# Low parts of the second weights: from VectorE subtractions to negated copies and adding transfers inside SBUF

## The chip, the cores and the metric

One core of a Trainium2 chip runs the whole kernel. The metric is the device time of one execution in microseconds (us); lower is better. The kernel before has a median of 1407.5 us over three executions.

## What is computed

Two transformer blocks in a row, each over 512 tokens of width 1024 (the second one has 16 more meta tokens inside it). Around the change only the MLP of each block matters:

```python
# first block
x = x + jnp.square(jax.nn.relu(h2 @ w_mlp_in[layer])) @ w_mlp_out[layer]
# second block
def squared_relu_mlp(u, w_ff1, w_ff2):
    hdn = jnp.square(jax.nn.relu(jnp.einsum('bld,df->blf', u, w_ff1)))
    return jnp.einsum('blf,fd->bld', hdn, w_ff2)
```

`w_mlp_in` and `w_ff1` are 1024 x 4096, `w_mlp_out` and `w_ff2` 4096 x 1024. The other parts (two attentions, a gated linear attention, norms, gates) are untouched.

## The kernel before, in words

**Split operands.** Every float32 operand of TensorE is kept as a high part (a copy rounded to `fp32r`) and a low part (operand minus high part). A product is three matmuls: high x high, high x low, low x high. So each weight costs an ACT copy (high part) and a VectorE subtraction (low part): `wh`, `wl` for what is read straight from a weight, `Sh`, `Sl` for blocks of the second weight.

**The MLPs.** Each of the two MLPs goes through the hidden dimension in 4 chunks of 1024. The last chunk of each is done in another way; the first three run in a loop on every engine (`strassen_chunk`), and only these are changed. One such chunk has two stages:

- *Slab stage*: 8 products of the first weight, each 24 matmuls of 128x512 (`products`, L2355). The last of them belongs to the next chunk.
- *Pair stage*: 4 pairs, q = 0 to 3, each 256 columns of the second weight. A pair is 7 block products in Strassen's manner (`block_product`, L2420), each 12 matmuls of 128x256, in this order: A11, S1, S2, S3, S4, A12, A22. A11, A12 and A22 are blocks of the weight itself; S1 to S4 are sums of blocks. A12 and A22 together are the pair's lower half, and A11 its upper left block.

So there are 2 MLPs x 3 chunks x 4 pairs = 24 pairs.

**Who makes what.** The raw weights (1 MB for two slabs or for a pair) come by SP's transfers into `raw`, which has two slots. A slot is loaded again when `lo_ready` says that the low parts of what lay in it are done (`mlp_loads`, L663). The sums S1 and S3 are made by GpSimd's queue: `s13_sums` issues two plain transfers of 256 KB (L824), waits for them (`s13_base`), and issues two adding transfers of 256 KB on top (L827). It runs for unit u = 4c + q, and waits first until the S1 and S3 of unit u - 2 have been split (`s13_lo`, the VectorE instruction L1550). S2 and S4 are VectorE additions (L1535, L1541).

The lower half of a pair is split by ACT L988 (high part, 128x1024, `hi_ready`) and VectorE L1568 (low part, `lo_ready`). ACT may start on it when the pair before has ended (`slab_done`), because `wh[:, 1]` is still read by that pair's A12 and A22. TensorE waits for it only ahead of A12. The upper left block is split by ACT L968 (`a11_hi`) and VectorE L1545 (`a11_lo`); it is needed at the start of a pair.

ACT, VectorE, GpSimd and SP each work through a program in fixed order, written by hand, with waits on semaphores; GpSimd's is `strassen_sums`.

Of the kernel before, what the change touches and what calls it, by code (L numbers as in the profile page):

```python
# [23 lines left out]
F32 = mybir.dt.float32  # L24
# [9 lines left out]
DM = 1024  # L34
# [137 lines left out]
def build(nc, d):  # L172
# [21 lines left out]
    with ctx:  # L194
# [41 lines left out]
        def region(at, *shape):  # L236
# [126 lines left out]
            sem("blk_done"), sem("mid_read"), sem("mids_zero"), sem("x_combined"))  # L363
        a11_hi, a11_lo, s13_hi, s13_lo = sem("a11_hi"), sem("a11_lo"), sem("s13_hi"), sem("s13_lo")
        s2_hi, s2_lo, s4_hi, s4_lo = sem("s2_hi"), sem("s2_lo"), sem("s4_hi"), sem("s4_lo")
        s13_base, s2_sum, s4_sum = sem("s13_base"), sem("s2_sum"), sem("s4_sum")
        s13_sum = sem("s13_sum0"), sem("s13_sum1")
        hid_sq, t_diff, t4_diff, hid_hi, hid_lo = (
            sem("hid_sq"), sem("t_diff"), sem("t4_diff"), sem("hid_hi"), sem("hid_lo"))
        g_landed, ts_sum, ts3_sum = sem("g_landed"), sem("ts_sum"), sem("ts3_sum")  # L370
        tw_hi, tw_lo, y_t = sem("tw_hi"), sem("tw_lo"), sem("y_t")
# [88 lines left out]
        def lower_pair(p):  # L460

            return raw[:, p % 2, :].rearrange("p (k n) -> p k n", k=KT)[:, 4:8, :].rearrange("p k (o n) -> p o k n", o=2)

        def lower_slot(w):

            return w[:, 1, :].rearrange("p (o k n) -> p o k n", o=2, k=4)

# [247 lines left out]
        def _(pool):  # L715
# [47 lines left out]
            def strassen_sums(which):  # L763
                t0, _, p0 = MLPS[which]
                pool.memset(mids, 0.0).then_inc(mids_zero, 1)
                if which == REAL:
                    add_squares(3, REAL)
                for c in range(CHUNKS - 1):
                    for q in range(4):
                        s13_sums(which, c, q)  # L770
                if which == REAL:
                    first_token_sum()
                pool.wait_ge(evac_done, t0 + 16 * (CHUNKS - 1))
                x = X[:, :, META:S2].rearrange("p (q o) (t n) -> p q o t n", o=2, t=2)
                n = 4 if which == REAL else 0
                pool.tensor_tensor(x[:, :, 0, 1], x[:, :, 0, 1], mids[:, :, 0:HB], ALU.add).then_inc(x_combined, 1)
                pool.tensor_tensor(x[:, :, 1, 0], x[:, :, 1, 0], mids[:, :, 0:HB], ALU.subtract).then_inc(x_combined, 1)
                pool.tensor_tensor(x[:, :, 1, 1], x[:, :, 1, 1], mids[:, :, 0:HB], ALU.subtract).then_inc(x_combined, 1)
                pool.wait_ge(x_combined, n + 3)
                pool.tensor_tensor(x[:, :, 1, 1], x[:, :, 1, 1], mids[:, :, HB:2 * HB], ALU.subtract).then_inc(x_combined, 1)  # L780
                pool.wait_ge(x_combined, n + 4)
                if which == REAL:
                    token_sums()

            def add_block(upper, left, accumulate, landed):
# [114 lines left out]
        def _(act):  # L900
# [52 lines left out]
            def strassen_chunk(which, c):  # L953
# [12 lines left out]
                def upper_left(q):  # L966
                    act.wait_ge(w_landed[(p0 + 4 + q) % 2], landed_count(p0, 4 + q) + 64 * c)
                    act.activation(blk(Sh[:, 0:S1]), quarter(p0 + 4 + q, 0, 0), ACT.Copy).then_inc(a11_hi, 1)  # L968

# [17 lines left out]
                def lower(q):  # L987
                    act.activation(lower_slot(wh), lower_pair(p0 + 4 + q), ACT.Copy).then_inc(hi_ready, 2)  # L988

# [448 lines left out]
        def _(dve):  # L1438
# [78 lines left out]
            def strassen_chunk(which, c):  # L1517
# [24 lines left out]

                def upper_left(q):
                    dve.wait_ge(a11_hi, pairs + q + 1)
                    dve.tensor_tensor(blk(Sl[:, 0:S1]), quarter(p0 + 4 + q, 0, 0), blk(Sh[:, 0:S1]),  # L1545
                                      ALU.subtract).then_inc(a11_lo, 1)

                def first_sums(q):
# [16 lines left out]

                def lower(q):
                    dve.wait_ge(hi_ready, t + 8 + 2 * q + 2)
                    dve.tensor_tensor(lower_slot(wl), lower_pair(p0 + 4 + q), lower_slot(wh), ALU.subtract)\  # L1568
                       .then_inc(lo_ready, 2)

# [9 lines left out]
                for j in range(8):  # L1580
# [25 lines left out]
                    else:  # L1606
# [6 lines left out]
                                                 op0=ALU.mult, op1=ALU.subtract).then_inc(t4_diff, 1)  # L1613
                        if j == 6:
                            upper_left(0)
                        if j == 7:
# [4 lines left out]
                        if j == 7:  # L1621
# [3 lines left out]
                                          hidden_part(Hh, k, T4, 3), ALU.subtract).then_inc(hid_lo, 1)  # L1625
                    if j == 7:
                        lower(0)

                for q in range(4):
                    g1, g2, g3, g4 = pair_banks(q)  # L1630
                    done, last = blocks + 6 * q, q == 3
                    x0, x1 = X[:, 2 * q, META:S2], X[:, 2 * q + 1, META:META + HB]
                    mid = halves(mids[:, q])
                    if q > 0:
                        first_mids(q)
                    dve.wait_ge(blk_done, done + 4)
                    dve.wait_ge(mid_read, reads + 2 * q + 1)
                    dve.tensor_tensor(mid, mid, ps[:, g2:g4 + 1, 0:HB], ALU.add).then_inc(mid_read, 1)
                    if last:
                        slab_weights(p0, 0, t + 17)  # L1640
                    else:
                        upper_left(q + 1)
                        second_sum(q + 1)
                        fourth_sum(q + 1)
                        first_sums(q + 1)
                    dve.wait_ge(blk_done, done + 6)
                    dve.tensor_tensor(halves(x0), halves(x0), ps[:, g1:g3 + 1, 0:HB], ALU.add)
                    if not last:
                        last_low(q + 1)
                    dve.wait_ge(slab_done, t + 8 + 2 * q + 2)  # L1650
                    dve.tensor_tensor(x1, x1, ps[:, g4, 0:HB], ALU.subtract).then_inc(evac_done, 2)
                    if last:
                        slab_weights(p0, 1, t + 18)
                    else:
                        lower(q + 1)

# [681 lines left out]
        def _(pe):  # L2338
# [66 lines left out]
            def strassen_chunk(which, c):  # L2405
# [4 lines left out]
                upper, lower = slice(0, S1), slice(S1, DM)  # L2410
                A12_, A22_ = (blk(wh[:, 1, upper]), blk(wl[:, 1, upper])), (blk(wh[:, 1, lower]), blk(wl[:, 1, lower]))
                S4_, S2_ = (blk(wh[:, 0, upper]), blk(wl[:, 0, upper])), (blk(wh[:, 0, lower]), blk(wl[:, 0, lower]))
# [16 lines left out]
                for q in range(4):  # L2429
                    g1, g2, g3, g4 = pair_banks(q)  # L2430
                    pe.wait_ge(a11_lo, pairs + q + 1)
                    if q == 0:
# [23 lines left out]
                    block_product(S4_, B22, g3, False, all_ready).then_inc(blk_done, 1)  # L2456
                    pe.wait_ge(lo_ready, t + 8 + 2 * q + 2)
                    block_product(A12_, B21, g1, False).then_inc(blk_done, 1)
# [529 lines left out]
```

## Time and profile before

| what | value |
|---|---|
| median of 3 executions | 1407.5 us (1407.33 to 1407.54) |
| the profiled execution, first to last instruction (span) | 1405.3 us |
| median less that span | 2.2 us |
| TensorE busy | 1397.8 us, 99% of the span |
| VectorE busy | 921.2 us, 66% |
| ACT busy | 596.3 us, 42% |
| GpSimd busy | 211.8 us, 15% |
| mean traffic | 115 GB/s, 161.61 MB |

The profiled execution has no separately recorded time; its span stands for it, and the 2.2 us between span and median are taken as a constant that lies around the span. Durations of single instructions overlap: a matmul of 128x256 is shown with 0.28 us, but the next one starts 0.12 us after it. So distances are read from starts, not from durations.

### The profile page before, as it was taken

What the parts mean: (1) busy time and instruction counts of PE and PEld (TensorE: products, weight loads), DVE (VectorE), ACT (ScalarE), POOL (GpSimd) and SP (SyncE); (2) the same over time, 40 slices, a digit from 0 to 9 for tenths busy, and PEclk for the clock granted to TensorE, in tenths of its full rate; (3) what the DMA queues carried; (4) which work ended last, traced back from release to release, by engine and by line L of the source; (5) the groups of instructions that cost most, each with busy time, mean ns of one, the idle gap of its engine ahead of it and who ended that gap; (6) DMA issues with size and microseconds to landing.
All of it is one profiled execution on the core that took longest, in us unless ns stands there. A gap on an engine that the chain in (4) does not pass through costs nothing.

```text
span 1405.3 us, 21789 instructions
## 1 busy us (share of the span) xinstructions
PE 1397.8 (99%) x8746; PEld 1184.5 (84%) x8746; DVE 921.2 (66%) x1248; ACT 596.3 (42%) x842; POOL 211.8 (15%) x215
## 2 busy tenths in 40 slices
PE   9999999999999999999999999999999999999998
PEld 7898779777888989989888997778888998989886
DVE  6635433765767858577656778556756967758775
ACT  4324531553445434353244435344434535344353
POOL 4000000000022302211433020000022221302310
PEclk9999999999999999999999999999999999999999
DMA  5223123211336845635233322232225773927573
GB/s 183 90 91 113 61 68 102 72 31 59 100 99 169 188 133 144 157 114 153 91 96 99 92 63 82 64 103 90 90 90 139 180 162 113 214 91 191 138 175 109
DMA packets 154860, 161.61 MB, mean 115 GB/s; under 512 B 4010, under 2 KB 144660, under 8 KB 154788
## 3 DMA queue, kind: packets, MB, share of 16 engines
q1 hardware_dynamic: 122868, 129.12, 28.9%
q0 software_dynamic: 31904, 31.46, 12.3%
q8 instruction: 53, 0.87, 0.3%
q14 instruction: 19, 0.16, 0.0%
q10 hardware_dynamic: 16, 0.00, 0.0%
HBM read 157.68 MB, written 2.10 MB: 114 GB/s over the span
## 4 chain that ended last, share of the span: by engine, by line
PE 99%; ACT 0%; DVE 0%; issue 0%; POOL 0%; POOLq 0%; ACTq 0%
PE ps L2355 63%; PE ps L2420 17%; PE ps L2351 4%; PE ps L2377 4%; PE ps L2493 3%; PE ps L2748 1%; PE ps L2563 1%; PE ps L2777 1%; PE ps L2763 1%; PE ps L2867 1%; PE ps L2652 0%; PE ps L2695 0%; PE ps L2674 0%; PE ps L2949 0%; PE ps L2540 0%; PE ps L2713 0%
## 5 line engine op out<-in xcount | busy, mean ns | idle before, releaser
L2355 PE MATMUL ps<-AA,wh 128*128 128x512 f32 x1440 | 453.5, 396 | 0.0
L2355 PE MATMUL ps<-BB,wh 128*128 128x512 f32 x1088 | 342.2, 396 | 0.2 <-issue 0.2
L2355 PEld LDWEIGHTS ps<-AA,wh 128*128 128x128 f32 x1440 | 267.4, 188 | 62.6 <-DVE wl L1449 0.8
L2355 PE MATMUL ps<-AA,wl 128*128 128x512 f32 x720 | 283.4, 394 | 0.0
L915 ACT ACTIVATE wh<-raw 128x1024 fp32r<-128x1024 f32 (+2 forms) x149 | 141.5, 950 | 259.8 <-PE ps L2355 206.0
L2355 PEld LDWEIGHTS ps<-BB,wh 128*128 128x128 f32 x1088 | 202.2, 188 | 49.3 <-issue 1.6
L2355 PE MATMUL ps<-BB,wl 128*128 128x512 f32 x544 | 213.9, 393 | 0.0
L1449 DVE TENSOR_TENSOR wl<-raw,wh 128x1024 fp32r<-128x1024 f32 (+2 forms) x149 | 169.9, 1140 | 60.6 <-ACT wh L915 60.3
L2355 PEld LDWEIGHTS ps<-AA,wl 128*128 128x128 f32 x720 | 135.4, 188 | 30.9
L2355 PEld LDWEIGHTS ps<-BB,wl 128*128 128x128 f32 x544 | 102.3, 188 | 23.3
L2420 PE MATMUL ps<-Hl,wh 128*128 128x256 f32 x384 | 107.8, 281 | 0.0
L1494 DVE TENSOR_TENSOR arena<-ps,RS 128x512 f32<-128x512 f32 (+2 forms) x55 | 37.9, 689 | 73.1 <-PE ps L2355 69.2
L1526 DVE TENSOR_TENSOR wl<-raw,wh 128x1024 fp32r<-128x1024 f32 x48 | 62.2, 1296 | 31.6 <-ACT wh L963 16.5
L2420 PE MATMUL ps<-Hl,Sh 128*128 128x256 f32 x288 | 81.1, 282 | 0.0
L2420 PEld LDWEIGHTS ps<-Hl,wh 128*128 128x128 f32 x384 | 72.3, 188 | 0.0
L963 ACT ACTIVATE wh<-raw 128x1024 fp32r<-128x1024 f32 x36 | 38.1, 1060 | 62.0 <-PE ps L2355 62.0
L1588 DVE SCALAR_TENSOR_TENSOR zf<-ps,RS 128x512 f32<-128x512 f32 x48 | 33.2, 691 | 44.9 <-PE ps L2355 44.2
L2420 PEld LDWEIGHTS ps<-Hl,Sh 128*128 128x128 f32 x288 | 54.2, 188 | 0.2
L2420 PE MATMUL ps<-AA,wh 128*128 128x256 f32 x192 | 54.3, 283 | 0.0
L2420 PE MATMUL ps<-AA,wl 128*128 128x256 f32 x192 | 53.8, 280 | 0.0
L2420 PE MATMUL ps<-BB,wl 128*128 128x256 f32 x192 | 53.7, 280 | 0.0
L2420 PE MATMUL ps<-BB,wh 128*128 128x256 f32 x192 | 53.7, 280 | 0.0
(408 smaller groups left out, 2410.6 us busy)
## 6 DMA issues: line engine op xcount, KB each, us to landing
raw<-in_w_in SPq DMA_DIRECT2D x38, 1024.0 KB, 5.4
raw<-in_w_ff SPq DMA_DIRECT2D x31, 1024.0 KB, 5.4
raw<-in_w_mlp_in SPq DMA_DIRECT2D x16, 1024.0 KB, 5.4
raw<-in_w_mlp_out SPq DMA_DIRECT2D x16, 1024.0 KB, 5.3
zf<-in_w_mlp_out POOLq DMA_DIRECT2D x48, 256.0 KB, 4.8
zf<-in_w_ff POOLq DMA_DIRECT2D x48, 256.0 KB, 4.6
raw<-in_w_out SPq DMA_DIRECT2D x8, 1024.0 KB, 5.4
arena<-in_x SPq DMA_DIRECT2D x4, 512.0 KB, 7.1
```

Source lines behind the costliest of these rows:

```text
L915: act.activation(w_slab(wh, t % 2, kt), raw_slab(t), ACT.Copy).then_inc(hi_ready, 1)
L963: act.activation(w_slab(wh, j % 2, KT), raw_half((p0 + i) % 2, j % 2, KT, 2), ACT.Copy)\
L1449: dve.tensor_tensor(w_slab(wl, t % 2, kt), raw_slab(t), w_slab(wh, t % 2, kt), ALU.subtract)\
L1494: dve.tensor_tensor(tokens(dst, kind), dense_psum(t, kind)[0:rows], tokens(scale, kind), ALU.mult)\
L1526: dve.tensor_tensor(w_slab(wl, slot, KT), raw_half(p % 2, slot, KT, 2), w_slab(wh, slot, KT), ALU.subtract).then_inc(lo_ready, 1)
L1588: dve.scalar_tensor_tensor(out=f, in0=halves(dense_psum(t0 + j, which)), scalar=0.0, in1=halves(RS[:, 0:S1]), op0=ALU.max, op1=ALU.mult).t ...
L2351: last = pe.matmul(dense_psum(t_ps, ALL)[:, half, :], a[:, k, :], b[:, o0 + k, half * HALF2:(half + 1) * HALF2], start=start, stop=stop)
L2355: last = pe.matmul(dense_psum(t_ps, kind), a[:, k, :], b[:, o0 + k, col0:col0 + S1], start=start, stop=stop)
L2377: mm = pe.matmul(ps[:, value_banks(t) + a // 2, a % 2 * 256:a % 2 * 256 + 256], x, w[:, k, :], start=(half == 0 and k == 0 and i == 0 and ...
L2420: mm = pe.matmul(ps[:, bank, 0:HB], w[:, k, :], hidden_part(x, k, b), start=(first and k == 0 and i == 0), stop=(k == 3 and i == 2), skip_ ...
L2493: mm = pe.matmul(ps[:, bank, :], x, v[:, k, :], start=(first and k == 0 and n == 0), stop=(k == 3 and n == 2), skip_group_check=True)
L2563: return pe.matmul(dense_psum(t, ONE), w_slab(w, t, KT)[:, k, :], x[:, k, 0:S1], start=first, stop=last)
```

## The change

Low parts of the lower half and of the upper left block are no longer VectorE subtractions. ACT writes, beside the high part, a second copy with scale -1 into the place of the low part (so that `wl` or `Sl` holds minus the high part, rounded as it is), and GpSimd's queue adds the raw weight onto it by a transfer from SBUF to SBUF with `accumulate`. The lower half keeps the layout of `raw` now, so that a partition's 1024 elements are one run on both sides; TensorE picks A12 and A22 out with a stride. The adding transfers are new entries in GpSimd's fixed order: after the sums of unit u come the lower half of unit u - 2 and the upper left block of unit u - 1. TensorE waits for their landings (`a11_landed`, `lower_lo`), and VectorE waits for `lower_lo` too, to pass it on as `lo_ready` to SP.

```diff
+        neg_hi, lower_lo = sem("neg_hi"), sem("lower_lo")
+        neg_a11, a11_landed = sem("neg_a11"), sem("a11_landed")
...
         def lower_pair(p):
-            return raw[:, p % 2, :].rearrange("p (k n) -> p k n", k=KT)[:, 4:8, :].rearrange("p k (o n) -> p o k n", o=2)
-
-        def lower_slot(w):
-
-            return w[:, 1, :].rearrange("p (o k n) -> p o k n", o=2, k=4)
+            return raw[:, p % 2, DM:2 * DM]
+
+        def lower_block(w, o):
+
+            return w[:, 1, :].rearrange("p (k o n) -> p o k n", o=2, k=4)[:, o]
...
                 for c in range(CHUNKS - 1):
                     for q in range(4):
                         s13_sums(which, c, q)
+                        if 4 * c + q >= 2:
+                            lower_low(which, 4 * c + q - 2)
+                        if 4 * c + q >= 1:
+                            upper_left_low(which, 4 * c + q - 1)
+                lower_low(which, 4 * (CHUNKS - 1) - 2)
+                upper_left_low(which, 4 * (CHUNKS - 1) - 1)
+                lower_low(which, 4 * (CHUNKS - 1) - 1)
...
+            def upper_left_low(which, u):
+                pool.wait_ge(neg_a11, so_far(which, 4) + u + 1)
+                pool.dma_start(blk(Sl[:, 0:S1]).bitcast(F32), quarter(MLPS[which][2] + 4 + u % 4, 0, 0), accum_op=ALU.add)\
+                    .then_inc(a11_landed, 16)
+
+            def lower_low(which, u):
+                pool.wait_ge(neg_hi, so_far(which, 4) + u + 1)
+                pool.dma_start(wl[:, 1, :].bitcast(F32), lower_pair(MLPS[which][2] + 4 + u % 4), accum_op=ALU.add).then_inc(lower_lo, 16)
...
                 def upper_left(q):
                     act.wait_ge(w_landed[(p0 + 4 + q) % 2], landed_count(p0, 4 + q) + 64 * c)
+                    act.activation(blk(Sl[:, 0:S1]), quarter(p0 + 4 + q, 0, 0), ACT.Copy, scale=-1.0).then_inc(neg_a11, 1)
                     act.activation(blk(Sh[:, 0:S1]), quarter(p0 + 4 + q, 0, 0), ACT.Copy).then_inc(a11_hi, 1)
...
                 def lower(q):
-                    act.activation(lower_slot(wh), lower_pair(p0 + 4 + q), ACT.Copy).then_inc(hi_ready, 2)
+                    act.activation(wh[:, 1, :], lower_pair(p0 + 4 + q), ACT.Copy).then_inc(hi_ready, 2)
+                    act.activation(wl[:, 1, :], lower_pair(p0 + 4 + q), ACT.Copy, scale=-1.0).then_inc(neg_hi, 1)
...
-                def upper_left(q):
-                    dve.wait_ge(a11_hi, pairs + q + 1)
-                    dve.tensor_tensor(blk(Sl[:, 0:S1]), quarter(p0 + 4 + q, 0, 0), blk(Sh[:, 0:S1]),
-                                      ALU.subtract).then_inc(a11_lo, 1)
...
-                def lower(q):
-                    dve.wait_ge(hi_ready, t + 8 + 2 * q + 2)
-                    dve.tensor_tensor(lower_slot(wl), lower_pair(p0 + 4 + q), lower_slot(wh), ALU.subtract)\
-                       .then_inc(lo_ready, 2)
+                def lower_landed(q):
+                    dve.wait_ge(lower_lo, 16 * (so_far(which, 4) + q + 1) + 64 * c)
+                    dve.sem_inc(lo_ready, 2)
...
                     else:
-                        upper_left(q + 1)
                         second_sum(q + 1)
                         fourth_sum(q + 1)
                         first_sums(q + 1)
+                    lower_landed(q)
                     dve.wait_ge(blk_done, done + 6)
...
-                A12_, A22_ = (blk(wh[:, 1, upper]), blk(wl[:, 1, upper])), (blk(wh[:, 1, lower]), blk(wl[:, 1, lower]))
+                A12_, A22_ = ((lower_block(wh, o), lower_block(wl, o)) for o in range(2))
...
-                    pe.wait_ge(a11_lo, pairs + q + 1)
+                    pe.wait_ge(a11_hi, pairs + q + 1)
+                    pe.wait_ge(a11_landed, 16 * (so_far(which, 4) + q + 1) + 64 * c)
...
-                    pe.wait_ge(lo_ready, t + 8 + 2 * q + 2)
+                    pe.wait_ge(lower_lo, 16 * (so_far(which, 4) + q + 1) + 64 * c)
                     block_product(A12_, B21, g1, False).then_inc(blk_done, 1)
```

**GpSimd's queue.** Before, from the sums of unit 2 of the first MLP on (L824 are the plain, L827 the adding transfers of `s13_sums`):

```order
L824 DMA zf<-in_w_mlp_out 128x4x128 [waits s2_sum,s13_lo]
L824 DMA zf<-in_w_mlp_out 128x4x128
L827 DMA zf<-in_w_mlp_out 128x4x128 [waits s13_base]
L827 DMA zf<-in_w_mlp_out 128x4x128
L824 DMA zf<-in_w_mlp_out 128x4x128 [waits s2_sum,s13_lo]
```

In the changed kernel the same place (L842 and L845 are these transfers now; L796 is the upper left block, L801 the lower half):

```order
L796 DMA Sl<-raw 128x4x128 [waits neg_a11]
L842 DMA zf<-in_w_mlp_out 128x4x128 [waits s2_sum,s13_lo]
L842 DMA zf<-in_w_mlp_out 128x4x128
L845 DMA zf<-in_w_mlp_out 128x4x128 [waits s13_base]
L845 DMA zf<-in_w_mlp_out 128x4x128
L801 DMA wl<-raw 128x1024 [waits neg_hi]
L796 DMA Sl<-raw 128x4x128 [waits neg_a11]
L842 DMA zf<-in_w_mlp_out 128x4x128 [waits s2_sum,s13_lo]
```

Each unit has two more transfers with a wait of their own, and they stand behind the four transfers of a later unit's sums and behind the wait in their midst.

**VectorE, end of the slab stage and first pair.** Before, from the last hidden low part to the reading of the middle results of pair 0 (L1568 is the lower half's low part of pair 0):

```order
L1624 TENSOR_TENSOR Hl<-zf,AA 128x768 [waits hid_hi]
L1567 REGISTER_ALU
L1568 TENSOR_TENSOR wl<-raw,wh 128x1024 [waits hi_ready]
L1636 REGISTER_ALU
L1638 TENSOR_TENSOR zf<-zf,ps 128x512 [waits mid_read,blk_done]
```

Changed, the same place and on to pair 0's results (L1648 was L1638, L1565 was L1550, L1656 is in `x0`'s line behind the wait for the landing, L1657 was L1647):

```order
L1636 TENSOR_TENSOR Hl<-zf,AA 128x768 [waits hid_hi]
L1646 REGISTER_ALU
L1648 TENSOR_TENSOR zf<-zf,ps 128x512 [waits mid_read,blk_done]
L1555 TENSOR_TENSOR zf<-zf,raw 128x512 [waits s13_sum1,w_landed1,s4_lo]
L1560 REGISTER_ALU [waits s4_lo]
L1561 TENSOR_TENSOR zf<-raw,zf 128x512 [waits s2_sum]
L1565 TENSOR_TENSOR Sl<-zf,Sh 128x1024 [waits s13_hi]
L1582 REGISTER_ALU
L1656 REGISTER_ALU [waits lower_lo]
L1657 TENSOR_TENSOR X<-X,ps 128x512 [waits blk_done]
```

The subtraction is gone, and a wait for the transfer's landing stands between the split of the next pair's S1 and S3 and the reading of this pair's results; what releases the slot of `raw` comes out of that wait.

## Rows read from the trace of the kernel before

**Rows 1.** Page, part 1: busy time, share of the span, instructions.

```profile
PE 1397.8 (99%) x8746; PEld 1184.5 (84%) x8746; DVE 921.2 (66%) x1248; ACT 596.3 (42%) x842; POOL 211.8 (15%) x215
```

**Rows 2.** Waits of TensorE: engine line <- releaser: us in total, times, longest.

```profile
PE ps L2555 <- POOL ident L726: 1.7, 1, 1.7
PE ps L2563 <- ACT AA L1169: 0.5, 1, 0.5
PE ps L2355 <- issue: 0.2, 1, 0.2
```

**Rows 3.** Stretches: us; busy of PE, PEld, DVE, ACT, POOL; PEclk; DMA share; GB/s.

```profile
460.00:470.00 10.00, 10.00 (x87) 10.00 (x86) 9.73 (x15) 6.51 (x9) 2.78 (x4) 1.00 0.75 159
480.00:490.00 10.00, 10.00 (x87) 10.00 (x86) 7.62 (x11) 3.19 (x3) 4.17 (x4) 1.00 0.94 212
500.00:510.00 10.00, 10.00 (x45) 8.11 (x44) 3.72 (x6) 3.30 (x5) 0.00 (x0) 1.00 0.33 105
```

**Rows 4.** Timeline of TensorE: start of pair 0, its A12, start of pairs 1 and 2.

```profile
457.65 0.28 PE L2420 MATMUL ps<-AA,Sh 128*128 128x256 f32 x1
...
464.76 0.28 PE L2420 MATMUL ps<-AA,wh 128*128 128x256 f32 x1
...
467.63 0.28 PE L2420 MATMUL ps<-AA,Sh 128*128 128x256 f32 x1
...
477.61 0.28 PE L2420 MATMUL ps<-AA,Sh 128*128 128x256 f32 x1
```

**Rows 5.** Timeline of ACT: high parts of the lower halves of pairs 0 and 2.

```profile
461.94 1.04 ACT L988 ACTIVATE wh<-raw 128x1024 fp32r<-128x1024 f32 x1
...
477.87 1.07 ACT L988 ACTIVATE wh<-raw 128x1024 fp32r<-128x1024 f32 x1 [0.53 <-PE ps L2420]
```

**Rows 6.** Timeline of VectorE: pair 0's lower half, pair 2's S1 and S3.

```profile
463.38 1.22 DVE L1568 TENSOR_TENSOR wl<-raw,wh 128x1024 fp32r<-128x1024 f32 x1
...
476.10 1.22 DVE L1550 TENSOR_TENSOR Sl<-zf,Sh 128x1024 fp32r<-128x1024 f32 x1
```

**Rows 7.** Timeline of GpSimd's queue, sums of units 3 and 4; idle time in brackets.

```profile
468.63 1.54 POOL L824 DMA_DIRECT2D zf<-in_w_mlp_out  x2 [7.22 <-DVE Sl L1550]
473.57 2.62 POOL L827 DMA_DIRECT2D zf<-in_w_mlp_out  x2 [3.39 <-DMA zf<-in_w_mlp_out]
477.62 1.54 POOL L824 DMA_DIRECT2D zf<-in_w_mlp_out  x2 [1.43 <-DVE Sl L1550]
```

**Rows 8.** Single lines: their issues (ns), and below each the time to landing.

```profile
L824 POOL DMA_DIRECT2D zf<-in_w_mlp_out x24: 777/778/1884, 419.2 to 638.2; - x24
...
DMA to landing us min/median/max: 3.3/3.5/10.6
...
L827 POOL DMA_DIRECT2D zf<-in_w_mlp_out x24: 1306/1562/1876, 425.7 to 642.8; - x24
...
DMA to landing us min/median/max: 4.2/5.3/10.7
...
L663 SPq DMA_DIRECT2D raw<-in_w_mlp_out x12: 372/373/382, 439.9 to 640.5; - x12
...
DMA to landing us min/median/max: 4.9/5.4/10.7
```

**Rows 9.** DMA queues, 470 to 490 us: packets, MB, share of 16 engines.

```profile
q0 software_dynamic: 2490, 2.32, 63.9%
q1 hardware_dynamic: 2080, 2.10, 31.9%
```

**Rows 10.** DMA queue of GpSimd, 1355 to 1367 us (one adding transfer of 1 MB).

```profile
q0 software_dynamic: 528, 1.05, 51.3%
```

**Rows 11.** VectorE's groups that the change removes: busy us, mean ns, idle.

```profile
L1568 DVE TENSOR_TENSOR wl<-raw,wh 128x1024 fp32r<-128x1024 f32 x24 | 29.2, 1217 | 0.0
...
L1545 DVE TENSOR_TENSOR Sl<-raw,Sh 128x512 fp32r<-128x512 f32 x24 | 16.4, 684 | 0.0
```

**Rows 12.** Waits of SP's queue.

```profile
SPq L663 <- DVE wl L1568: 197.0, 20, 14.9
```

More of the change, by code:

```diff
@@ L363, in build @@
             sem("blk_done"), sem("mid_read"), sem("mids_zero"), sem("x_combined"))
-        a11_hi, a11_lo, s13_hi, s13_lo = sem("a11_hi"), sem("a11_lo"), sem("s13_hi"), sem("s13_lo")
+        a11_hi, s13_hi, s13_lo = sem("a11_hi"), sem("s13_hi"), sem("s13_lo")
         s2_hi, s2_lo, s4_hi, s4_lo = sem("s2_hi"), sem("s2_lo"), sem("s4_hi"), sem("s4_lo")
@@ L1613, in strassen_chunk @@
                                                  op0=ALU.mult, op1=ALU.subtract).then_inc(t4_diff, 1)
-                        if j == 6:
-                            upper_left(0)
                         if j == 7:
@@ L1625, in strassen_chunk @@
                                           hidden_part(Hh, k, T4, 3), ALU.subtract).then_inc(hid_lo, 1)
-                    if j == 7:
-                        lower(0)
                 for q in range(4):
@@ L1653, in strassen_chunk @@
                         slab_weights(p0, 1, t + 18)
-                    else:
-                        lower(q + 1)
             def mlp_last():
```

## The prediction

> **What bounds the kernel now.** I read the page's busy times first, then TensorE's waits, then stretches of the pair stage, then the timelines of one pair engine by engine, and last the DMA queues. TensorE is busy for 1397.8 us of 1405.3 [rows 1], and all its waits in the whole program are 1.7, 0.5 and 0.2 us [rows 2]: none of them lies at the block products. In the pair stage it starts as many matmuls (x87 in 10 us) whether VectorE is busy for 9.73 or for 7.62 of the 10 us [rows 3]. So TensorE has nothing to gain from a freer VectorE, neither a wait nor pace. Whatever the change delays beyond its cover is added to the time, and nothing of it is made good later, as TensorE has no idle time to eat into.
>
> The cover is short. A pair starts at 457.65, its A12 at 464.76, the next pairs at 467.63 and 477.61 [rows 4]: a pair lasts 10.0 us, and the lower half is due 7.1 us after its start. ACT begins the high part of pair 0's lower half at 461.94, late, behind its work on the hidden parts; for pair 2 it begins at 477.87, 0.26 us into the pair [rows 5]. VectorE then has the low part of pair 0 done at 464.60, just ahead of 464.76 [rows 6].
>
> **What the change removes.** 24 subtractions of 1.217 us and 24 of 0.684 us on VectorE, 45.6 us of busy time [rows 11]. On the path they are worth nothing, as said. Their one effect is that pair q+1's S1 and S3 are split some 0.6 us earlier in pair q: now the split ends at 476.10 + 1.22 = 477.3, which is 9.7 us after the pair's start, then about 9.1.
>
> **What it adds on ACT.** Per pair a negated copy of 128x1024 (1.06 us, as the high part in rows 5) and one of 128x512. ACT is idle for over half of a pair stage's stretch, 3.19 busy of 10 us in the later pairs [rows 3], so they cost nothing on ACT itself, but the first one stands in series ahead of the transfer.
>
> **What it adds on the queues.** Per pair one adding transfer of 512 KB for the lower half and one of 256 KB for the upper left block. No row shows one from SBUF to SBUF. What it costs has two sides, engine time and landing.
>
> *Engine time.* In 470 to 490 us the loads took 31.9% of 20 us for 2.10 MB, the sums' queue 63.9% for 2.32 MB [rows 9]. A load of 1.05 MB is thus 3.2 us of all 16 engines, a pair's sums (1.05 MB) 5.8 us. Half of the sums is plain; at the loads' rate that half is 1.6 us, which leaves 4.2 us for the adding half, 8.0 us per MB. The one adding transfer of 1 MB, whose runs are 2 KB long instead of 512 B, took 51.3% of 12 us for 1.05 MB, 5.9 us per MB [rows 10]. The lower half has runs of 4 KB, so I take 5.9 for it: 0.52 MB, 3.1 us. The upper left block has runs of 512 B, so 8.0: 0.26 MB, 2.1 us. Bounds for the two: 1.6 and 0.8 us at the loads' rate, 4.2 and 2.1 at 8.0 us per MB.
>
> *Landing.* A load lands after 5.4 us [rows 8], 2.2 more than its 3.2 of engine time. So the lower half lands 2.2 + 3.1 = 5.3 us after its issue when nothing else runs; bounds 3.8 and 6.4. The nearest rows agree: 5.3 in the median for adding transfers of 256 KB two at a time, 3.5 for plain ones [rows 8]. The Trainium skill, "DMA: Bandwidth & Descriptors", section on the anatomy of one DMA on the SWDGE path, gives about 2.0 us plus bytes over 436 GB/s whatever the transfer does: 3.2 us for 512 KB. This trace contradicts it for adding transfers, whose 256 KB take longer than plain ones; by it the sum below would be 34 us instead of 86.
>
> **The sum, per chunk.** *Pair 0.* ACT's high part ends at 462.98, the negated copy at about 464.0, the landing at 469.3; A12 was due at 464.76. TensorE waits 4.5 us.
>
> *Pairs 1 to 3.* All 16 engines now have 3.2 (load) + 5.8 (sums) + 3.1 + 2.1 = 14.2 us of work per pair, against 9.0 before, where a pair lasts 10.0 and the DMA share was already 0.94 [rows 3]. GpSimd's order ties every pair to all of it: the lower half of unit u - 2 is issued behind unit u's sums. The same loop followed through the waits: from a pair's start 9.1 us to the split of S1 and S3, 1.5 for two plain issues, 3.4 until they land, 2.6 for two adding issues [rows 7], 5.3 for the landing of the next pair's lower half, 2.9 for A12 and A22. That is 24.8 us for two pairs, 12.4 for one, if nothing shares the engines. The larger one holds, about 14.1 us a pair: 4.1 us of waiting in each of three pairs, and 4.5 + 12.3 = 16.8 us in chunks 1 and 2 of each MLP.
>
> *Chunk 3* has no sums of a further chunk to issue, so the lower halves of its pairs 2 and 3 stand behind nothing. The landing is at 0.26 + 2.0 + 5.3 = 7.6 us into the pair, 0.5 late. Together 4.5 + 4.1 + 0.5 + 0.5 = 9.6 us.
>
> One MLP: 2 x 16.8 + 9.6 = 43.2 us; two: 86.4 us. Against the profiled span 1405.3 + 86.4 = 1491.7; the medians lie 2.2 above the span, so **1493.9**.
>
> Edits costed at nothing: the upper left block is issued 1.3 us behind a lower half and due 2.9 us after that one's A12 may start, so it lands under A12 and A22; without that cover it would cost up to 2 us a pair. VectorE's new wait for the landing stands ahead of reading a pair's results (due only two pairs later, by `evac_done`) and of S4's low part for the next pair, needed 2.9 us into it; the landing that VectorE waits for is one TensorE waits for anyway. SP gets a slot of `raw` some 8 us later than now, but it now lies idle for 197 us in 20 waits behind that release, 10 us each [rows 12], and the load (5.4 us) is needed in the next pair but one's preparation. The strided choice of A12 and A22 still reads runs of 128 elements.
>
> **Rivals.**
> *B, cheap transfers.* From SBUF to SBUF an adding transfer costs what a load does per byte. For it: no HBM is read. Against it: adding costs 2.6 times a load's rate where it is seen. Engine work is then 11.4 us a pair and the loop (24.8 - 1.5)/2 = 11.7: 1.7 us a pair, 3.0 in pair 0, nothing in the tail. Chunks 8.1, 8.1 and 4.7, in all 42 us: 1449. The skill's formula, told above, belongs here too and gives 1441 to 1442.
> *C, dear transfers.* The lower half pays 8.0 us per MB, or the queues slow each other. 15.3 us a pair, 5.6 in pair 0, 1.6 in the tail: chunks 21.5, 21.5 and 14.1, in all 114 us: 1522. For it: the longest landings of single lines are 10.6 and 10.7 us [rows 8].
> *D, the clock.* The granted clock is 1.00 in every stretch shown [rows 3], but TensorE never pauses there for 4 us. If pauses bring it down to 1.2 GHz, matmuls behind them start 0.24 us apart instead of 0.12. Were that so through all 24 pairs it would add up to 240 us; for a part of them, 1550 or more. The Trainium skill, "TensorE: Matmul & The Clock Gate", Part 1, says that idleness halves the clock; no row here shows it.
> *E, not slower.* The table of waits is kept: every landing comes before its A12. This needs pair 0's transfer to land within 0.8 us of its issue (464.0 to 464.76) and the others within 4.7, or TensorE's wait to pass before the landing. From 0.8 us on in pair 0 it decides the other way. The shortest landing seen is 3.3 us [rows 8]. It would give 1407.5, or at best some 4 us less if matmuls started 1% closer without VectorE's reads, which rows 3 speak against.
>
> **How the numbers follow.** Forecast (A) 0.62, B 0.20, C 0.13, D 0.03, E 0.02. The likeliest is A: 1494. The range reaches from B's 1449 to just past C's 1522, 1530, as C's cause could be sharing that I can't price; it leaves out D, E and the edges of B and C. Slower by over 0.2% (2.8 us, about what a measurement of this kernel can tell from no change) is A to D, 0.98; E is split evenly between no change and faster.
>
> **What would show it.** In the profile after: TensorE's waits list the first matmul of A12, released by a transfer into `wl`, some 24 times and 80 to 90 us in all, nearly nothing for `Sl`; waits near 4.5 us in pair 0, near 4 in pairs 1 to 3 and near 0.5 in the last two pairs of each MLP; pairs of 14 us with a DMA share of 0.95 or more; transfers into `wl` landing after 5 to 7 us; the slab stage as before at 5.6 us a slab; a clock of 1.00. I am wrong if the DMA share stays under 0.9 while pairs still stretch (then GpSimd's order alone is the bound), or if TensorE waits for the upper left block or for S4 instead.

## The result, and the profile after

The changed kernel takes 1517.5 us in the median of four executions (1513.1 to 1523.2), against 1407.5: 110 us more, a ratio of 1.078 with a 95% interval of 1.076 to 1.081. The profiled execution is the longest of the four, 1521.5 us from first to last instruction; a span lies 1.7 us under its execution's time here. So 116.2 us are to be found in the trace, and 110 is the difference of the medians.

The page of the kernel after, its busy times of TensorE and, below, what TensorE waited for (us in total, times, longest):

```profile
PE 1441.6 (95%) x8746; PEld 1222.4 (80%) x8746; DVE 886.3 (58%) x1200; ACT 630.7 (41%) x890; POOL 264.5 (17%) x263
```

```profile
PE ps L2428 <- DMA wl<-raw: 72.1, 21, 6.7
PE ps L2564 <- POOL ident L728: 1.7, 1, 1.7
PE ps L2363 <- DVE wl L1469: 0.5, 1, 0.5
PE ps L2363 <- issue: 0.2, 1, 0.2
```

Before, this table held 2.4 us in all [rows 2]. Now it has one more row, and it is the one foretold: TensorE waits 72.1 us, 21 times, for transfers into `wl`, and never for `Sl`. Busy time has grown too, from 1397.8 [rows 1] to 1441.6, with the same x8746 matmuls. 72.1 + 43.8 = 115.9 us: all but 0.3 of the 116.2. What the 43.8 us are, the next two views say. First the timeline of TensorE, the A12 of pairs 0 to 3 of the first chunk, with the wait ahead of each in brackets:

```profile
469.14 0.58 PE L2428 MATMUL ps<-AA,wh 128*128 128x256 f32 x1 [3.94 <-DMA wl<-raw]
469.52 0.42 PE L2428 MATMUL ps<-Hl,wh 128*128 128x256 f32 x1
469.73 0.42 PE L2428 MATMUL ps<-AA,wl 128*128 128x256 f32 x1
...
483.89 0.39 PE L2428 MATMUL ps<-AA,wh 128*128 128x256 f32 x1 [2.19 <-DMA wl<-raw]
...
488.36 0.28 PE L2428 MATMUL ps<-AA,Sh 128*128 128x256 f32 x1
...
500.33 0.58 PE L2428 MATMUL ps<-AA,wh 128*128 128x256 f32 x1 [4.73 <-DMA wl<-raw]
...
515.50 0.58 PE L2428 MATMUL ps<-AA,wh 128*128 128x256 f32 x1 [2.79 <-DMA wl<-raw]
```

The pairs' waits are 3.94, 2.19, 4.73 and 2.79 us. The line of 488.36 is the start of pair 2. And behind the first of them matmuls start 0.21 us apart (469.52, 469.73) where they started 0.12 us apart in rows 4. The stretches around it, with the granted clock (PEclk) third from the right; the last one lies behind pair 1's wait:

```profile
458.00:465.00 7.00, 7.00 (x61) 6.99 (x59) 6.43 (x11) 5.32 (x8) 3.25 (x4) 1.00 0.59 80
465.00:469.00 4.00, 0.20 (x2) 0.00 (x0) 2.01 (x3) 2.03 (x3) 2.95 (x4) 0.83 0.90 152
469.00:474.00 5.00, 4.86 (x22) 4.86 (x23) 1.82 (x2) 0.00 (x0) 0.20 (x1) 0.50 1.07 236
475.00:481.00 6.00, 6.00 (x53) 6.00 (x53) 1.53 (x4) 3.49 (x5) 4.87 (x4) 1.00 0.96 153
486.00:488.00 2.00, 2.00 (x11) 2.00 (x11) 1.80 (x2) 0.00 (x0) 0.00 (x0) 0.50 1.09 378
```

Up to 465 TensorE is busy throughout, from 465 to 469 for 0.20 us, and from 469 to 474 the clock is 0.50, the 1.2 GHz level; by 475 it is back at 2.4 GHz. It is at 0.50 again from 486 to 488, behind pair 1's wait of only 2.19 us. A12 and A22 together take 5.3, 4.5, 5.1 and 4.4 us in the four pairs, where they took 2.9 [rows 4]: 7.8 us more in this chunk. Over six chunks, two of which have such waits in two pairs only, that is about the size of the 43.8 us of busy time. The Trainium skill, "TensorE: Matmul & The Clock Gate", Part 1, says that idleness halves the clock; this trace agrees, with 0.50 behind the wait of 3.94 us.

Last, the transfers: the lines' times to landing, the SBUF transfers (L801, L796) and the sums' plain ones (L842), and then GpSimd's queue from pair 1 to pair 3:

```profile
L801 POOL DMA_DIRECT2D wl<-raw x24: 872/1576/2027, 464.4 to 1420.2; - x24
...
DMA to landing us min/median/max: 4.6/6.9/7.8
...
L796 POOL DMA_DIRECT2D Sl<-raw x24: 1275/1645/2765, 452.2 to 1410.5; - x24
...
DMA to landing us min/median/max: 4.2/6.7/9.4
...
L842 POOL DMA_DIRECT2D zf<-in_w_ff x24: 777/790/1866, 1122.0 to 1386.6; - x24
...
DMA to landing us min/median/max: 3.5/5.4/10.5
```

```profile
483.97 1.55 POOL L842 DMA_DIRECT2D zf<-in_w_mlp_out  x2 [4.09 <-DVE Sl L1565]
491.76 2.64 POOL L845 DMA_DIRECT2D zf<-in_w_mlp_out  x2 [6.24 <-DMA zf<-in_w_mlp_out]
493.31 2.00 POOL L801 DMA_DIRECT2D wl<-raw  x1
...
497.66 1.54 POOL L842 DMA_DIRECT2D zf<-in_w_mlp_out  x2 [1.03 <-DVE Sl L1565]
506.72 2.64 POOL L845 DMA_DIRECT2D zf<-in_w_mlp_out  x2 [7.52 <-DMA zf<-in_w_mlp_out]
508.27 2.00 POOL L801 DMA_DIRECT2D wl<-raw  x1
```

The plain transfers landed after 3.5 us in the median before [rows 8] and take 5.4 now; GpSimd waits 7.52 us for them in pair 2. Before, its waits for them in pairs 1 to 3 were 3.39 [rows 7], 3.04 and 3.01.

### The profile page after: what moved, and what is told of

Read it like the earlier page. It is cut to its first block, busy times and chain, and to the rows that moved or that the text cites. A ratio compares the mean times of both kernels' runs of the same rounds, so it can differ in the third digit from the quotient of the medians.

```text
span 1521.5 us, 21843 instructions
## 1 busy us (share of the span) xinstructions
PE 1441.6 (95%) x8746; PEld 1222.4 (80%) x8746; DVE 886.3 (58%) x1200; ACT 630.7 (41%) x890; POOL 264.5 (17%) x263
## 4 chain that ended last, share of the span: by engine, by line
PE 82%; DMA 10%; ACT 2%; DVE 2%; POOL 2%; issue 1%; ACTq 0%; DVEq 0%; SPq 0%; POOLq 0%
PE ps L2363 58%; PE ps L2428 6%; DMA wl<-raw 5%; PE ps L2359 4%; PE ps L2385 4%; PE ps L2502 3%; DMA zf<-in_w_ff 2%; DMA zf<-in_w_mlp_out 2%; POOL zf L845 1%; PE ps L2757 1%; PE ps L2786 1%; DVE Sl L1565 1%; PE ps L2772 1%; PE ps L2876 1%; POOL zf L842 1%
## 5 line engine op out<-in xcount | busy, mean ns | idle before, releaser
L2363 PEld LDWEIGHTS ps<-AA,wh 128*128 128x128 f32 x1440 | 267.5, 188 | 63.9 <-DVE wl L1469 2.3
L2363 PEld LDWEIGHTS ps<-BB,wh 128*128 128x128 f32 x1088 | 202.2, 188 | 49.2 <-issue 1.4
L2428 PE MATMUL ps<-Hl,wh 128*128 128x256 f32 x384 | 123.8, 322 | 0.0
L2428 PE MATMUL ps<-BB,wh 128*128 128x256 f32 x192 | 64.4, 336 | 35.9 <-DMA wl<-raw 35.9
L2428 PE MATMUL ps<-AA,wh 128*128 128x256 f32 x192 | 63.0, 328 | 36.2 <-DMA wl<-raw 36.2
L2428 PEld LDWEIGHTS ps<-Hl,wh 128*128 128x128 f32 x384 | 89.2, 232 | 0.0
L1514 DVE TENSOR_TENSOR arena<-ps,RS 128x512 f32<-128x512 f32 (+2 forms) x55 | 38.0, 691 | 73.1 <-PE ps L2363 69.1
L796 POOL DMA_DIRECT2D Sl<-raw x24 | 42.0, 1748 | 218.5 <-ACT Sl L986 218.3
L1546 DVE TENSOR_TENSOR wl<-raw,wh 128x1024 fp32r<-128x1024 f32 x48 | 60.5, 1261 | 31.4 <-ACT wh L981 16.2
L2428 PEld LDWEIGHTS ps<-BB,wh 128*128 128x128 f32 x192 | 45.0, 235 | 38.4 <-DMA wl<-raw 38.4
L2428 PEld LDWEIGHTS ps<-AA,wh 128*128 128x128 f32 x192 | 43.7, 227 | 38.6 <-DMA wl<-raw 38.5
L1007 ACT ACTIVATE wh<-raw 128x1024 fp32r<-128x1024 f32 x24 | 25.4, 1057 | 109.7 <-PE ps L2428 109.7
L1657 DVE TENSOR_TENSOR X<-X,ps 128x512 f32<-128x512 f32 x24 | 16.5, 688 | 85.2 <-PE ps L2428 85.2
```

Source lines behind the costliest of these rows:

```text
L796: pool.dma_start(blk(Sl[:, 0:S1]).bitcast(F32), quarter(MLPS[which][2] + 4 + u % 4, 0, 0), accum_op=ALU.add)\
L1007: act.activation(wh[:, 1, :], lower_pair(p0 + 4 + q), ACT.Copy).then_inc(hi_ready, 2)
L1514: dve.tensor_tensor(tokens(dst, kind), dense_psum(t, kind)[0:rows], tokens(scale, kind), ALU.mult)\
L1546: dve.tensor_tensor(w_slab(wl, slot, KT), raw_half(p % 2, slot, KT, 2), w_slab(wh, slot, KT), ALU.subtract).then_inc(lo_ready, 1)
L2363: last = pe.matmul(dense_psum(t_ps, kind), a[:, k, :], b[:, o0 + k, col0:col0 + S1], start=start, stop=stop)
L2428: mm = pe.matmul(ps[:, bank, 0:HB], w[:, k, :], hidden_part(x, k, b), start=(first and k == 0 and i == 0), stop=(k == 3 and i == 2), skip_ ...
```

## Experiments

Each was run beside the kernel before on the same chip. "Waits" is TensorE's time in waits beyond the 2.4 us it had, "busy" its busy time beyond 1397.8 us, both from the profiled execution.

| kernel | us (median) | ratio, 95% interval | waits | busy | mean clock |
|---|---|---|---|---|---|
| the change | 1517.5 | 1.078 (1.076 to 1.081) | 72.1 | 43.8 | 0.967 |
| e1_upper_only | 1445.5 | 1.028 (1.026 to 1.031) | 26.1 | 8.2 | 0.998 |
| e2_lower_only | 1512.7 | 1.075 (1.072 to 1.078) | 69.1 | 35.2 | 0.973 |
| e3_reordered | 1495.7 | 1.063 (1.061 to 1.065) | 55.6 | 31.1 | 0.981 |
| e4_tiny | 1488.0 | 1.058 (1.056 to 1.060) | 54.2 | 26.4 | 0.979 |
| e7_reordered_tiny | 1437.4 | 1.021 (1.019 to 1.022) | 22.9 | 9.3 | 0.998 |
| e10_sums_plain | 1484.7 | 1.056 (1.054 to 1.057) | 48.1 | 28.4 | 0.978 |
| e9_reordered_neg_first | 1492.9 | 1.059 (1.056 to 1.062) | 64.8 | 29.3 | 0.979 |
| e6_refill_before | 1477.5 | 1.049 (1.048 to 1.051) | 0 | 70.7 | 0.999 |
| e5_refill2 | 1529.3 | 1.085 (1.083 to 1.088) | 35.5 | 86.2 | 0.989 |
| e8_refill_some | 1520.4 | 1.081 (1.079 to 1.083) | 55.9 | 57.3 | 0.984 |

In the profiled executions of e4, e5, e7 and e9 the waits hold one of 4.1 to 5.1 us that is no landing: TensorE waits for VectorE's L1546, and one instruction of that line takes 8.5 to 9.5 us there instead of 1.2. What holds it up is open; so up to 5 us of the waits in these four rows may not belong to their edits.

**Which half of the change: e1 and e2.** e1 gives the lower half back to VectorE (its low part in the new layout, released to SP once the upper left block's transfer has landed as well):

```diff
-                        if 4 * c + q >= 2:
-                            lower_low(which, 4 * c + q - 2)
...
-                    act.activation(wl[:, 1, :], lower_pair(p0 + 4 + q), ACT.Copy, scale=-1.0).then_inc(neg_hi, 1)
...
+                    dve.wait_ge(hi_ready, t + 8 + 2 * q + 2)
+                    dve.wait_ge(a11_landed, 16 * (so_far(which, 4) + q + 1) + 64 * c)
+                    dve.tensor_tensor(wl[:, 1, :], lower_pair(p0 + 4 + q), wh[:, 1, :], ALU.subtract)\
+                       .then_inc(lo_ready, 2)
...
-                    pe.wait_ge(lower_lo, 16 * (so_far(which, 4) + q + 1) + 64 * c)
+                    pe.wait_ge(lo_ready, t + 8 + 2 * q + 2)
```

> Only the upper left block goes by negated copy and adding transfer; the lower half's low part is VectorE's again. Theory A (the 16 DMA engines' work sets the length of a pair): 3.2 + 5.8 + 2.1 = 11.1 us of work per pair instead of 14.2, so about 1 us of waiting a pair at most: 1420 to 1432. Theory Q (GpSimd's order sets it): the block of pair p + 2 is issued behind the sums of unit p + 3, 16.7 us after the start of pair p, lands 4.7 to 5.3 later and is due at 20: 1 to 2 us per two pairs, 1420 to 1430 too, with the waits at the first matmul of a pair. Theory N (the upper left block is covered): 1407.5, and then nearly all of the 110 us is the lower half's.

e2 is the other half, `upper_left_low` and its negated copy out, VectorE's `upper_left` back.

> Only the lower half goes by negated copy and adding transfer; the upper left block's low part is VectorE's again. Theory A: 12.1 us of engine work per pair instead of 14.2, so the waits of pairs 1 to 3 fall by about 2 us each, some 28 us in all plus what the clock gives back: 1475 to 1490. Theory Q: the lower half stands behind the same sums as before and lands when it did; only the 1.3 to 2 us issue of the other transfer is gone: 1500 to 1517.

Measured: 1445.5 and 1512.7. TensorE's waits in e1:

```profile
PE ps L2428 <- DMA Sl<-raw: 26.1, 16, 3.2
```

e1 costs 38 us, more than any theory gave it: the waits at the first matmul of pairs 1 to 3 (1.44, 3.21 and 0.82 us in the first chunk) are those of theory Q, but larger, as the block lands after 5.6 us in the median, behind the sums issued just ahead of it. (In e1 VectorE waits for the same landings, 7.5 us in all, which it does not in the whole change.) Alone it costs 38 us, yet taking it out of the whole change saves 5, with intervals that overlap, so perhaps nothing. So the two halves don't add up. The reading that fits is that they hang on the same loop and the lower half's wait hides the other, as TensorE never waits for `Sl` in the whole change. e2 speaks for Q and against A: 2.1 us less engine work per pair gave nearly nothing back.

**Order or engine work: e3, e4 and e7.** e3 moves the new transfers ahead of the wait for the plain ones:

```diff
                 pool.dma_start(blk(sums[:, s]), rows[0:S1, at].rearrange("(k p) n -> p k n", p=P)).then_inc(s13_base, 16)
+                if 4 * c + q >= 2:
+                    lower_low(which, 4 * c + q - 2)
+                if 4 * c + q >= 1:
+                    upper_left_low(which, 4 * c + q - 1)
                 pool.wait_ge(s13_base, 32 * u + 32)
```

(Their places behind the sums, in the loop over the units, are taken out.)

> The whole change, but in GpSimd's order the lower half of unit u - 2 and the upper left block of unit u - 1 stand between the plain and the adding transfers of unit u, not behind them. Theory A: the engines have the same 14.2 us of work per pair, so it stays over 1495. Theory Q: the lower half no longer waits for the sums to land nor stands behind 4.2 us of adding; it lands about 7.6 us into a pair, 0.5 us late in pairs 1 to 3 and 4.5 in pair 0, some 35 us in all: 1440 to 1450, if the clock holds.

e4 keeps the order and shrinks what moves, here for the lower half and in the same way for the upper left block:

```diff
-                pool.dma_start(wl[:, 1, :].bitcast(F32), lower_pair(MLPS[which][2] + 4 + u % 4), accum_op=ALU.add).then_inc(lower_lo, 16)
+                pool.dma_start(wl[:, 1, 0:16].bitcast(F32), lower_pair(MLPS[which][2] + 4 + u % 4)[:, 0:16], accum_op=ALU.add).then_inc(lower_lo, 16)
```

> The whole change, but both new transfers move only 16 of a partition's elements, so the low parts lack the raw weight elsewhere. Same order, same waits, nearly no engine work. Theory A: work per pair is back at 9.0 us, pairs 1 to 3 wait 1 us or less, pair 0 some 1.5 to 2 us (the landing of a tiny transfer is 2 to 2.5 us): 1420 to 1432. Theory Q (order and fixed landings alone): the loop still holds 9.1 + 1.5 + 3.4 + 2.6 + 2.3 + 2.9 = 21.8 us for two pairs, 0.9 us a pair: also under 1435, but if the sums' transfers alone keep the lower half waiting as now, over 1480.

e7 does both.

> The new order of e3 together with the tiny transfers of e4 (the low parts lack most of the raw weight). What is left is ACT's two copies in series and a landing of 2 to 2.5 us: pair 0 waits 1.3 to 2 us, pairs 1 to 3 nothing. 6 x 1.7 = 10 us: 1415 to 1420 by every theory that prices order and engine work alone; over 1430 would mean a wait none of them has.

Measured: 1495.7, 1488.0 and 1437.4. Order alone takes away 22 us, engine work alone 30, both together 80. Neither theory alone gives this; of e4's expectation the last branch came, over 1480. A stretch of e3 in the pair stage, then e4's landings of `wl`, then GpSimd's queue in e4 and the busy share of the 16 engines from 498 to 508 us, in 40 slices of 0.25 us:

```profile
470.00:510.00 40.00, 34.57 (x250) 33.96 (x248) 15.90 (x21) 13.05 (x15) 14.37 (x14) 0.87 1.05 213
```

```profile
L801 POOL DMA_DIRECT2D wl<-raw x24: 847/878/2007, 464.0 to 1379.6; - x24
...
DMA to landing us min/median/max: 2.0/3.3/5.5
```

```profile
493.79 1.57 POOL L842 DMA_DIRECT2D zf<-in_w_mlp_out  x2 [4.99 <-DVE Sl L1565]
499.47 2.64 POOL L845 DMA_DIRECT2D zf<-in_w_mlp_out  x2 [4.11 <-DMA zf<-in_w_mlp_out]
501.02 2.00 POOL L801 DMA_DIRECT2D wl<-raw  x1
...
DMA  4000000000000047999999999999632100000007
```

With the order mended, the 16 engines are full (share 1.05) and a pair lasts 12.8 to 14.0 us from A12 to A12, near theory A's 14.2: their work is then the bound, and e7, which takes it away, confirms it. With the transfers shrunk, the order is the bound, but not as I had it: a transfer of 8 KB in all, issued at 501.02 behind two adding ones, is what TensorE's A12 waits for until 506.52. The shortest landing is 2.0 us, the ones right behind the sums take up to 5.5. The engines are busy, almost wholly for GpSimd's queue, from 501.5 to about 505.5, and only then does the small one land. So in this kernel a transfer in GpSimd's queue stands behind the engine work of those issued before it, however small it is. A smaller part is issue: behind the sums it takes 2.00 us instead of 0.88. e4's expectation had given it 2.3 us there.

What e7 has left are 20 waits of 0.5 to 1.4 us, 18.8 us, the one of 4.6 us on VectorE that was told above, and 9.3 us of busy time. Its pair stage keeps the clock at 1.00, here from 460 to 512 us:

```profile
PE ps L2428 <- DMA wl<-raw: 18.8, 20, 1.4
PE ps L2363 <- DVE wl L1546: 4.6, 1, 4.6
...
460.00:512.00 52.00, 47.86 (x367) 45.67 (x367) 28.42 (x40) 23.51 (x28) 18.84 (x19) 1.00 0.75 175
```

I had expected no waits in pairs 1 to 3. There the transfer is issued while the plain ones of a later unit are still moving, and lands after 5.2 us in the median.

**What stands ahead in the queue: e10.** The sums' two later transfers lose their `accum_op=ALU.add`, and so, by the estimate below, more than half of their engine work:

```diff
-                                   .rearrange("(k p) n -> p k n", p=P), accum_op=ALU.add).then_inc(s13_sum[q % 2], 16)
+                                   .rearrange("(k p) n -> p k n", p=P)).then_inc(s13_sum[q % 2], 16)
```

> The whole change in its own order, but the two adding transfers of every unit's sums are plain (the sums then hold only their second block, so the output is another). Their engine work falls from 4.2 to about 1.6 us a unit, their issue and place in the queue stay. Theory Q (each transfer in GpSimd's queue stands behind the engine work of those before it): the lower half lands 2 us or more sooner after its issue, the plain sums sooner too, some 4 us per loop of two pairs: 1470 to 1490. If a landing behind others is a fixed cost that has nothing to do with their work: 1510 or more.

Measured: 1484.7, within theory Q's range. The landings of `wl` in e10, ahead of them the sums' issues, one MLP's:

```profile
L845 POOL DMA_DIRECT2D zf<-in_w_mlp_out x24: 749/749/757, 425.6 to 673.3; - x24
...
L801 POOL DMA_DIRECT2D wl<-raw x24: 872/912/952, 464.1 to 1380.9; - x24
...
DMA to landing us min/median/max: 4.6/4.9/5.5
```

Nothing of the new transfers changed, yet they land after 4.9 us in the median and 5.5 at most, where the change has 6.9 and 7.8. So the landing is made of 4.6 us of its own, the smallest seen in both, and of what stands in front, for the most part the adding transfers. The edit did more than its expectation said, though: the sums' issues fell as well, from 1.57 us in the median to 0.75, and the new transfer's own issue from 1.58 to 0.91. Some 0.7 of the 2.0 us are thus issue time, and e10 does not part the two; e4's engines, busy until a microsecond before the landing, show that the engine work is there.

**The series ahead of the transfer: e9.** On top of e3, ACT writes the negated copy first and TensorE waits for `hi_ready` too.

> The new order of e3, and ACT writes the negated copy before the high part, so the lower half's transfer can be issued one ACT copy (0.96 us) earlier; TensorE waits for the high part too. Pair 0, which hangs on nothing but ACT's copies and the landing, waits 1 us less in each of the 6 chunks. Pairs 1 to 3: in e3 the share of the 16 engines was 1.05 in the pair stage, so if their work bounds it (theory A, 13 to 14 us a pair) they gain nothing: 1485 to 1491. If the series ahead of the transfer bounds them, all 24 gain 1 us: 1468 to 1474.

Measured: 1492.9, with an interval that overlaps e3's: no gain that can be told. Its executions lie further apart than the others' (1485.4 to 1501.0), and the profiled one is the longest. Pair 0's wait fell from 3.85 to 3.09 us in the first chunk, about as expected, but the pairs behind it gave it back, with the engines at a share of 1.01:

```profile
470.00:510.00 40.00, 31.72 (x242) 31.19 (x241) 16.67 (x22) 13.52 (x15) 13.87 (x14) 0.89 1.01 210
```

**The clock: e5, e6 and e8.** Work is put where TensorE waits, to keep it from falling idle:

```diff
+                    for _ in range(2):
+                        block_product(S4_, B22, g3, False, all_ready)
                     block_product(S4_, B22, g3, False, all_ready).then_inc(blk_done, 1)
```

> The whole change, and S4's product is issued three times instead of once in every pair (the output then holds two more of it): 24 more matmuls, 2.85 us at full clock, just ahead of the wait for the lower half. Theory C (pauses of 2 to 7 us bring the clock down to 1.2 GHz, which costs some 40 of the 110 us): the pauses shrink under 1 to 2 us in most pairs, the clock stays at 1.00, and the kernel gets faster with 68 us more work: 1480 to 1500. Theory W (the time is the landings' alone, the clock costs nothing extra as the lower half is late anyway): 1515 to 1525, as the extra work fits the waits except in the last pairs of each MLP.

e6 is the same edit to the kernel before.

> The kernel before with the same 24 more matmuls per pair (output changed in the same way). It prices them where there is no wait to hide them: 24 pairs x 24 x 0.119 us = 68.5 us, so 1476, clock 1.00.

e8 puts it only where the waits are longest: `range((2, 1, 1, 0)[q])`.

> The whole change with S4's product issued three times in pair 0, twice in pairs 1 and 2 and once in pair 3 (the output holds more of it): 48 more matmuls a chunk, 6 x 5.7 = 34 us of work at full clock, placed where the waits were longest. If the halved clock costs net time (theory C in its weak form: each pair after a long pause pays for slow matmuls in the loop), the kernel is faster than the change alone although it does more: 1500 to 1513. If what the clock gives back is only waited out elsewhere in the loop (theory W), it is 1517 or more, up to 1525 with what doesn't fit.

Measured: 1529.3, 1477.5 and 1520.4. e6 prices the work at 70 us. In the changed kernel the same work costs 12, a little over what either theory gave e5. The waits in e5:

```profile
PE ps L2428 <- DMA wl<-raw: 31.4, 17, 4.9
```

The waits shrink from 72.1 to 31.4 us, the busy time beyond the added work from 43.8 to 86.2 - 70.7 = 15.5 us, the mean clock rises to 0.989. So the pauses do bring the clock down, and filling them keeps it up. But theory C was wrong in its size: neither e5 nor e8 is faster than the change. In e8 34 us of work cost 3, with intervals that overlap, and where a fill shortened pair 0's wait from 3.94 to 1.06 us, pair 1's grew from 2.19 to 3.90. Over the whole of e8 the slow matmuls shrank by some 20 us (43.8 to 57.3 - 34), but the waits fell by 16, not by the 34 of the work that was put into them. So what the clock gives back is mostly waited out at the next landing. This does not say what the slow matmuls cost net, as a clock that stays up without added work can't be had here; that part is left open.

## Why the prediction was right, and where it was not

Slower, and within 1449 to 1530; but 110 us against 86, a fifth too little. The waits themselves came to less than forecast, 72.1 us against 86, and 43.8 us came on top that the sum had at nothing: matmuls at the lower clock. That the total still lies in the range is in part luck. The range reached past 1494 for rival C's sake, and C's dear lower half did not occur: its shortest landing is 4.6 us, where C needed 6.4. C's other cause, queues that slow each other, is near to what the runs showed, but it stood there without a price. Rival B's cheap transfers fell with the same row, as B needed 3.8.

*TensorE has nothing to gain.* Right. VectorE's busy time fell from 921 to 886 us (35, not the 45.6 that the sum of the removed instructions gave) and no run was faster than before.

*Pair 0.* Forecast 4.5 us, measured 3.94; the landing was put at 5.3, and the shortest is 4.6. *The last two pairs of each MLP*: forecast 0.5 each, measured none, none, none and 0.48. *ACT at no cost, S4 and the upper left block covered*: right in the change, though e1, with waits of up to 3.2 us for that block, shows that its cover is only the other half's wait.

*Pairs 1 to 3.* This is the step that failed. I had two lengths for a pair, 14.1 us from the engines' work and 12.4 from the loop through GpSimd's order, and took the larger. Pairs 1 to 3 of the first chunk lasted 14.8, 16.4 and 15.2 us from A12 to A12 (469.14, 483.89, 500.33, 515.50), while the engines' share was not full; here it is for 484 to 516 us in 40 slices:

```profile
DMA  9599999300008999999999998999410998999940
```

They stand still for some 3 us around 492 and 1 us around 508, between the end of the plain transfers and the start of the adding ones, while GpSimd sees the landing and issues; for most of the rest they are full. The loop was mis-sized, term by term, with VectorE's split of S1 and S3 as its middle mark:

```profile
496.14 1.22 DVE L1565 TENSOR_TENSOR Sl<-zf,Sh 128x1024 fp32r<-128x1024 f32 x1
```

| term of the loop of two pairs | forecast, us | measured, us |
|---|---|---|
| A12 and A22 (483.89 to 488.36) | 2.9 | 4.5 |
| next pair's start to the split of S1 and S3 (to 497.36) | 9.1 | 9.0 |
| plain transfers issued and landed (to 506.72) | 4.9 | 9.4 |
| adding issues and landing of the lower half (to 515.50) | 7.9 | 8.8 |
| sum | 24.8 | 31.6 |

The largest error is the third row: I took the plain transfers' landing from a queue that held only sums [rows 7], when the change puts 5.2 us of adding work ahead of them. I had added that work to the engines' total and not to the landings it stands in front of. The true statement joins both of my theories: engine work counts in series wherever GpSimd's order makes one transfer wait for those before it. The first row is the clock. Over all six chunks the 14 pairs of this kind waited 3.4 us each, less than the 4.1 forecast; the slow matmuls make up the rest of their stretch.

*The clock.* Given 0.03 as a rival of its own, of 1550 us or more. It did happen, as a part of the likeliest case rather than instead of it, and its size was overrated. Nor did it need pauses of 4 us, as D had it: the clock was down behind pauses of 2.19 to 4.73 us. *The sign of my being wrong* was named rightly, a share under 0.9 while the pairs stretch: 484 to 516 us has 0.86 (469 to 520 us has 0.91). What it was to mean, that GpSimd's order alone is then the bound, went too far: e3 mends the order and gets back only 22 us.

## What to carry to other kernels

Before work is moved from an engine to a transfer, follow the loop that the transfer joins: what its queue must issue before it, and how much engine time that stands in front of it; a landing time read from a lightly used queue is the lower end. Where TensorE has no waits, relieving another engine gains nothing, and new waits can also cost matmuls at half the clock, as those of 2.2 us and more in the first chunk did here, while e7's of up to 1.4 us did not. Two bounds that are near each other (12.4 and 14.1 us here) need not combine to their maximum; where one feeds the other, as here, look for more than either.

## What the runs showed of the hardware that was not expected

An adding transfer of 64 bytes per partition took up to 5.5 us to land behind two adding transfers of 256 KB, and 2.0 us at the shortest (e4). From SBUF to SBUF, 512 KB added in runs of 4 KB landed after 4.6 us at least, 256 KB in runs of 512 B after 4.2 us, no faster than the 4.2 us of the same size from HBM [rows 8]. Without their adding, the issue of the sums' transfers took 0.75 us instead of 1.57 (e10). TensorE's clock was at 1.2 GHz behind pauses of 2.19 to 4.73 us amid dense work, and behind one of 3.21 us in e1 (0.50 from 484 to 486 us), with matmuls of 256 columns 0.21 us apart instead of 0.12. And matmuls worth 70 us, laid for the most part into TensorE's waits, cost 12 us.
